# A hybrid residual block on one core: modulation columns of the first stage in two halves, and the output stage's rows and sums shared out anew

## The chip, the cores and the metric

The kernel runs on one core of one Trainium2 chip. The metric is the device time of one execution in microseconds. A run is compared by the median of its executions.

## The reference, cut to what matters

One residual block for a sequence of T = 1024 tokens with D = 1024 channels. Two places matter here, its beginning and its end:

```python
ada = jax.nn.silu(c) @ w_ada[l] + b_ada[l]              # c: (1, 1024), w_ada: (1024, 6144)
sh1, sc1, gt1, sh2, sc2, gt2 = jnp.split(ada, 6, axis=-1)
h = layer_norm(x, ln_in_g, ln_in_b)
u = h * (1.0 + sc1[:, None, :]) + sh1[:, None, :]
...                                                      # u @ w_in, mixers, router, experts
ff = hier_moe(...)                                       # two expert results per token, weighted and added
h = layer_norm(DEEPNORM_ALPHA * h + gt2[:, None, :] * ff, ln2_g[l], ln2_b[l])
return h
```

Between them stand the attention and delta-rule branches, the merge, the router and the experts, which take most of the time and which the change leaves alone.

## The kernel before

The kernel is a chain of stages in one program; each engine has its instruction list written out by hand, with semaphores between them, and a barrier of all engines ends a stage. The SyncE queue (SP) issues nearly all loads, in the order of the text, and a transfer that stands behind others in that queue lands behind them.

**First stage** (`prepare`, lines 225 to 439). It normalises x, computes the first two of the six modulation rows (shift and scale), turns the tokens into channels (the transposed `u`, split into two float16 parts) and sums the keys of the attention. SP loads x in four transfers, then the 8 MB of `w_ada` columns 0 to 2047 in five transfers of whole rows (L272), then the first piece of `w_in` (`load_dense(0)`: 256 key and value columns, L170, and 16 narrow columns, L171), then small tables, the rest of the constant table (L276) and the next piece of `w_in`. VectorE takes the statistics of all eight token tiles (L390), then one square root on ScalarE, then ScalarE normalises the eight tiles in place (L359). The shift row is summed on TensorE as a 1-row product: for each of 8 blocks k of 128 channels two matmuls with one column of weights (L295). The scale row is summed on VectorE (L404, L407), reduced over partitions by TensorE (L335), and both are turned into columns (L302, L335) and folded with the layer norm's weights into `modulation` by five small VectorE instructions (L414 to L421). Only when this is done for all 1024 channels may the first of sixteen steps n (channel block k = n // 2, token half n % 2) be modulated. A step is: `turn(n)`, four transposes on TensorE (L311); the modulation on ScalarE (L371, L373) for the even n and on VectorE (L427) for the odd n; a cast on ScalarE (L377) and a subtraction on VectorE (L433) that make the two float16 parts; and `keys(n)`, three matmuls (L321). After step 1 VectorE makes the low half of the first `w_in` piece (`split_dense_low`, L190, 2176 columns), and keys(0) waits for it. TensorE's order is ada of k = 0 to 5, three turns, ada of 6 and 7, the columns, then turn(n) and keys(n - 4) by turns. The product for the relative bias (L346) stands after keys(4) there.

**Output stage** (the end of `experts`). For each of eight tiles c of 128 tokens SP loads the two expert results (1 MB, L2274 to L2277, a ring of four); TensorE adds them into two PSUM banks with an identity matrix (L2415: eight passes of 512 columns a tile); VectorE multiplies the sum by the gate row into a buffer `gated` (L2602), adds the residual and takes the row sum (`sums`, L2605, L2607); ScalarE squares, takes the root (`moments`, L2514, L2516); VectorE makes the reciprocal and the shift, a product of two one-column operands (`scalars`, L2611, L2613); ScalarE makes the unit tile (`unit`, L2522); VectorE multiplies by the scale row and adds the shift row (`scale`, L2617, L2619); SP stores (L2280). VectorE's order is sums(c), scalars(c - 1), scale(c - 2). GpSimd has no work in this stage.

Of the kernel before, what the change touches and what calls it, by code (L numbers as in the profile page):

```python
# [15 lines left out]
P = 128  # L16
# [149 lines left out]
def load_dense(m, a, sp, i):  # L166

    w = a["w_in"][0].rearrange("(k p) n -> p k n", p=P)
    if i == 0:
        sp.dma_start(m.w_ring[:, 0, :, 0:2 * P], w[:, :, KB0:KB0 + 2 * P]).then_inc(m.w_in[0], 16)  # L170
        sp.dma_start(m.w_ring[:, 0, :, 2 * P:], w[:, :, BA0:BA0 + 16]).then_inc(m.w_in[0], 16)  # L171
    else:
        at = QB0 + (i - 1) * 2 * P if i < 5 else (i - 5) * 2 * P
        sp.dma_start(m.w_ring[:, i % 2, :, 0:2 * P], w[:, :, at:at + 2 * P]).then_inc(m.w_in[i % 2], 16)


def split_dense_high(nc, m, act, i, quarter=None):

    n = WIDE if i == 0 else 2 * P
# [5 lines left out]
def split_dense_low(nc, m, dve, i, quarter=None):  # L185

    n = WIDE if i == 0 else 2 * P
# [37 lines left out]
def prepare(nc, m, a):  # L225

    ROW = (1, 7)
    ON_TENSOR = 2
    GROUPED = ((0, 1), (2, 3), (4, 5), (6,), (7,))
    with ExitStack() as ctx:  # L230
# [4 lines left out]
        ada = m.sb("ada_early", [P, 2 * KC], ctx=ctx)  # L235
        ada_row = m.sb("ada_early_row", [1, D], ctx=ctx)
        part = m.sb("ada_early_partial", [P, D], ctx=ctx)
# [11 lines left out]
        wada_in = [m.sem(f"w_ada_in{n}") for n in range(len(GROUPED))]  # L249
        vecs_t, vecs_ok, sig_ok, silu_ok, ada_mm, part_ok, cols_mm = (m.sem(n) for n in (  # L250
            "vecs_transposed", "vecs_ready", "sig_c_ready", "silu_c_ready", "ada_summed", "ada_partial_ready", "ada_columns"))
        row_ok = [m.sem(f"ada_row_ready{n}") for n in range(2)]
# [12 lines left out]
        def _(sp):  # L265
# [19 lines left out]
        def _(pe):  # L285
# [6 lines left out]
            def ada(k):  # L292
                pe.wait_ge(wada_in[k // 2 if k < 6 else k - 3], 16)
                for n in range(ON_TENSOR):
                    last = pe.matmul(ps[0:1, ROW[n], :], m.silu_c[:, k:k + 1], wada[:, k, n * 512:(n + 1) * 512], start=(k == 0), stop=(k == KC - 1))  # L295
                    if k == KC - 1:
                        last.then_inc(ada_mm, 1)

            def columns(n):
                pe.wait_ge(row_ok[n], 1)  # L300
                for j in range(4 * n, 4 * n + 4):
                    last = pe.transpose(ps[:, 6, j:j + 1], ada_row[0:1, j * P:(j + 1) * P], m.const("ident")[0:1, 0:1])  # L302
                last.then_inc(cols_mm, 1)
# [10 lines left out]
            def keys(n):  # L314

                k, half = n // 2, n % 2
                if n == 0:
                    pe.wait_ge(m.w_lo, 4)
# [8 lines left out]
            for k in range(KC):  # L327
                ada(k)
                if k == KC - 3:
                    pe.wait_ge(z_ok, TC)  # L330
                    for n in range(3):
                        turn(n)
            pe.wait_ge(part_ok, 1)
            for j in range(KC):
                last = pe.matmul(ps[:, 6, KC + j:KC + j + 1], part[:, j * P:(j + 1) * P], m.const("ones")[:, 0:1], start=True, stop=True)  # L335
            last.then_inc(cols_mm, 1)
            for n in range(ON_TENSOR):
                columns(n)
            turn(3)
            for n in range(4, 2 * KC):  # L340
                turn(n)
                keys(n - 4)
                if n == 8:
                    pe.wait_ge(rel_in, 16)
                    pe.wait_ge(rest_in, 16)
                    pe.matmul(ps[0:QH, 7, 0:320], rel[:], m.const("one_hot", BUCKETS), start=True, stop=True).then_inc(bias_mm, 1)  # L346
            for n in range(2 * KC - 4, 2 * KC):
                keys(n)

        @block.scalar  # L350
        def _(act):
            act.wait_ge(vecs_ok, 1)
            nc.scalar.activation(sig_c[:], m.vec("c"), ACT.Sigmoid).then_inc(sig_ok, 1)
            act.wait_ge(var_ok, 1)
            nc.scalar.activation(std[:], mv[:, :, 1], ACT.Sqrt, bias=eps[:, 0:1]).then_inc(std_ok, 1)

            act.wait_ge(shift_ok, 1)
            for c in range(TC):
                nc.scalar.activation(x[:, c, :], x[:, c, :], ACT.Identity, scale=rstd[:, c:c + 1], bias=shift[:, c:c + 1]).then_inc(z_ok, 1)  # L359
            act.wait_ge(ada_mm, 1)  # L360
            nc.scalar.copy(ada_row[:, 0:512], ps[0:1, ROW[0], :]).then_inc(row_ok[0], 1)
            split_dense_high(nc, m, act, 0)

            act.wait_ge(ada_ok, 1)
            for n in range(2 * KC):
                k, half = n // 2, n % 2
                if half == 0:
# [12 lines left out]
        def _(dve):  # L380
# [5 lines left out]
            nc.vector.tensor_tensor(m.silu_c[:], sig_c[:], m.vec("c"), ALU.mult).then_inc(silu_ok, 1)  # L386
            for c in range(TC):
                dve.wait_ge(x_in[c // 2], 16)
                for s in range(2):
                    step(nc.vector.bn_stats(stats[:, c, s, :], x[:, c, s * 512:(s + 1) * 512]))  # L390
# [9 lines left out]
            for k in range(KC):  # L400
# [7 lines left out]
                if k < KC - 1:  # L408
                    step(last)
# [2321 lines left out]
```

## Time and profile before

| | |
|---|---|
| median of 3 runs (lowest, highest) | 1876.89 us (1872.59, 1880.91) |
| the profiled execution | 1877.39 us |
| its span | 1875.3 us |
| first stage, start to the barrier behind it | 0 to 67.4 us |
| output stage, last expert store to the end | 1815 to 1875.3 us |
| PE, DVE, ACT, POOL busy over the span | 93%, 76%, 56%, 20% |

Times in the trace are microseconds from the start of the span. PE is TensorE, DVE VectorE, ACT ScalarE, POOL GpSimd, SP SyncE; a "q" behind the name is the engine's queue, which issues transfers. "L2415" is line 2415 of the kernel. A timeline row gives start, duration, engine, line, operation, output<-input, count, and in brackets the idle time before it with what ended it. The chain of waits is followed back from the last instruction: what it waited for, and so on.

### The profile page before, as it was taken

What the parts mean: (1) busy time and instruction counts of PE and PEld (TensorE: products, weight loads), DVE (VectorE), ACT (ScalarE), POOL (GpSimd) and SP (SyncE); (2) the same over time, 40 slices, a digit from 0 to 9 for tenths busy, and PEclk for the clock granted to TensorE, in tenths of its full rate; (3) what the DMA queues carried; (4) which work ended last, traced back from release to release, by engine and by line L of the source; (5) the groups of instructions that cost most, each with busy time, mean ns of one, the idle gap of its engine ahead of it and who ended that gap; (6) DMA issues with size and microseconds to landing.
All of it is one profiled execution on the core that took longest, in us unless ns stands there. A gap on an engine that the chain in (4) does not pass through costs nothing. (4 is left out here: it accounts for less than half of the span.)

```text
span 1875.3 us, 35089 instructions
## 1 busy us (share of the span) xinstructions
PE 1739.5 (93%) x14040; PEld 968.8 (52%) x14040; DVE 1427.8 (76%) x1786; ACT 1057.4 (56%) x1336; POOL 375.2 (20%) x261
## 2 busy tenths in 40 slices
PE   4999999999969999989999998599999999999975
PEld 1656664444448888744444455344554455444432
DVE  5646577968777889456766688799999988988938
ACT  3455663454444445342334211488888888888834
POOL 0000000111113434200000000124544444445300
PEclk9999999999989999999999998699999999999987
DMA  8500018663456232061223121699999999999945
GB/s 341 103 29 24 23 41 312 239 205 105 179 131 155 66 92 53 2 216 57 85 84 113 45 90 56 261 390 393 408 408 409 408 400 402 394 395 382 366 153 196
DMA packets 160711, 385.05 MB, mean 205 GB/s; under 512 B 24859, under 2 KB 102292, under 8 KB 132670
## 3 DMA queue, kind: packets, MB, share of 16 engines
q1 hardware_dynamic: 145982, 351.58, 51.7%
q0 software_dynamic: 14592, 31.56, 4.4%
q8 instruction: 96, 1.57, 0.4%
q14 instruction: 41, 0.34, 0.1%
HBM read 354.86 MB, written 48.15 MB: 215 GB/s over the span
## 5 line engine op out<-in xcount | busy, mean ns | idle before, releaser
L2351 PE MATMUL ps<-w_gate_up_split,gathered_t 128*128 128x512 f16 x1680 | 378.8, 382 | 2.0 <-ACT gathered_t L2438 1.2
L2538 DVE SCALAR_TENSOR_TENSOR w_gate_up_split<-w_staged,w_gate_up_split 128x2048 f16<-128x2048 f32 x138 | 314.3, 2289 | 48.6 <-ACT w_gate_up_split L2429 47.1
L2429 ACT ACTIVATE w_gate_up_split<-w_staged 128x2048 f16<-128x2048 f32 x136 | 259.1, 1908 | 29.9 <-PE ps L2351 16.4
L2351 PEld LDWEIGHTS ps<-w_gate_up_split,gathered_t 128*128 128x128 f16 x1680 | 163.5, 99 | 197.3 <-issue 9.4
L219 PE MATMUL ps<-u_transposed,w_gates_split 128*128 128x512 f16 x1152 | 253.7, 382 | 4.7 <-PEq L144 3.1
L840 PE MATMUL ps<-u_transposed,w_dense_split 128*128 128x512 f16 x1104 | 240.2, 379 | 0.8 <-PEq L452 0.8
L219 PEld LDWEIGHTS ps<-u_transposed,w_gates_split 128*128 128x128 f16 x1152 | 113.1, 98 | 144.9 <-issue 12.1
L2378 PE MATMUL ps<-w_down_split,hidden_t 128*128 128x512 f16 x816 | 183.5, 381 | 0.8 <-ACT hidden_t L2475 0.6
L840 PEld LDWEIGHTS ps<-u_transposed,w_dense_split 128*128 128x128 f16 x1104 | 107.2, 98 | 135.5 <-issue 7.8
L2538 DVE SCALAR_TENSOR_TENSOR w_down_split<-w_staged,w_down_split 128x2048 f16<-128x2048 f32 x68 | 155.1, 2287 | 10.8 <-ACT w_down_split L2429 10.4
L2429 ACT ACTIVATE w_down_split<-w_staged 128x2048 f16<-128x2048 f32 x68 | 129.6, 1909 | 37.0 <-DMA w_staged<-in_w_down 21.5
L2378 PEld LDWEIGHTS ps<-w_down_split,hidden_t 128*128 128x128 f16 x816 | 78.4, 98 | 91.4 <-issue 2.5
L2308 POOL DMA_INDIRECT slots_scratch<-block_output,slot_row_now x35 | 47.1, 1346 | 321.0 <-ACT block_output L2447 290.3
L1772 ACT ACTIVATE gate_sigmoids<-ps 128x1024 f32<-128x1024 f32 x24 | 24.4, 1023 | 143.9 <-PE ps L219 143.8
L966 DVE SCALAR_TENSOR_TENSOR delta_output<-w_gates_split,vector_columns,delta_output 128x1024 f32<-128x1024 f32 x66 | 84.3, 1283 | 21.4 <-ACT delta_output L904 19.8
L501 PE MATMUL ps<-u_transposed,w_dense_split 128*128 128x512 f16 x384 | 91.0, 383 | 0.0
L1099 POOL DMA_DIRECT2D qkv_scratch<-delta_output x20 | 11.1, 554 | 366.1 <-ACT delta_output L911 366.1
L1706 PE MATMUL ps<-w_out_split,delta_output 128*128 128x512 f16 x384 | 84.0, 379 | 0.0
L2009 POOL COPY slot_token_now<-slot_tokens 128x2 uint32<-128x2 uint32 x1 | 0.2, 188 | 417.8 <-DVEq L2099 417.8
L2294 POOL DMA_INDIRECT gathered<-u_scratch,slot_token_now x33 | 75.6, 2290 | 28.1 <-POOL slot_token_now L2291 28.1
L2304 POOL COPY slot_row_now<-slot_rows_index 128x1 uint32 (+1 forms) x35 | 72.5, 2071 | 1.7 <-issue 1.6
L897 ACT ACTIVATE w_gates_split<-ps 128x1024 f32<-128x1024 f32 x24 | 24.5, 1019 | 84.2 <-PE ps L840 82.0
(367 smaller groups left out, 2949.0 us busy)
## 6 DMA issues: line engine op xcount, KB each, us to landing
w_staged<-in_w_gate SPq DMA_DIRECT2D x70, 1024.0 KB, 11.5
w_staged<-in_w_up SPq DMA_DIRECT2D x70, 1024.0 KB, 10.7
w_staged<-in_w_down SPq DMA_DIRECT2D x70, 1024.0 KB, 10.7
w_dense_ring<-in_w_in SPq DMA_DIRECT2D x17, 1024.0 KB, 7.8
w_ada_ring<-in_w_ada SPq DMA_DIRECT2D x8, 2048.0 KB
w_gates_ring<-in_w_in SPq DMA_DIRECT2D x24, 512.0 KB, 6.1
qkv_scratch<-delta_output POOLq DMA_DIRECT2D x20, 512.0 KB, 5.2
attention_output<-qkv_scratch SPq DMA_DIRECT2D x8, 1024.0 KB, 7.3
```

Source lines behind the costliest of these rows:

```text
L219: last = pe.matmul(m.ps[:, 2 * j + half, :], m.gate16[n % 2][:, j, wp, k, :], m.u[:, up, k, half * 512:half * 512 + 512], start=(t == 0), ...
L501: last = pe.matmul(ps[:, bank, :], w16[:, i % 2, wp, k, (j % 2) * P:(j % 2 + 1) * P], m.u[:, up, k, half * 512:half * 512 + 512], start=(t ...
L840: last = pe.matmul(ps[:, 2 * (1 - b) + half, :], w16[:, (FIRST + p) % 2, i, k, b * P:(b + 1) * P], m.u[:, j, k, half * 512:half * 512 + 51 ...
L966: last = nc.vector.scalar_tensor_tensor(acc[:, b, :], raw[:, b, 1 + t:1 + t + T], conv[:, t, n:n + 1], acc[:, b, :], ALU.mult, ALU.add)
L1706: last = pe.matmul(ps[:, y_bank(c) + half, :], merged(k, op)[:, c * P:(c + 1) * P], m.w_out[:, wp, k, half * 512:half * 512 + 512], start= ...
L2294: pool.indirect_dma_start(xg[:, s].rearrange("p h d -> p (h d)"), None, m.u2_dram.rearrange("t h d -> t (h d)"), bass.IndirectOffsetOnAxis ...
L2304: nc.gpsimd.tensor_copy(row[:, s:s + 1], m.slot_row[:, bass.ds(n, 1)]).then_inc(S("row_ready"), 1)
L2308: pool.indirect_dma_start(m.y_dram, bass.IndirectOffsetOnAxis(ap=row[:, s:s + 1], axis=0), y[:, s, :], None, bounds_check=2 * T - 1, oob_i ...
L2351: last = pe.matmul(ps[:, GU[s] + j, :], xt[:, s, xp, k, :], w16[:, j, wp, k, :], start=(k == 0 and t == 0), stop=(k == KC - 1 and t == 2))
L2378: last = pe.matmul(ps[:, 6 + half, :], ht[:, s, hp, k, :], w[:, wp, k, half * 512:half * 512 + 512], start=(k == 0 and t == 0), stop=(k == ...
L2429: nc.scalar.activation(split(kind, 0, int(q)), staged(m, kind, int(q)), ACT.Identity, scale=W_SCALE).then_inc(hi_ok[kind + q], 1)
L2538: nc.vector.scalar_tensor_tensor(split(kind, 1, int(q)), staged(m, kind, int(q)), W_SCALE, split(kind, 0, int(q)), ALU.mult, ALU.subtract) ...
```

## The change

In the first stage (the first diff; `GROUPED` is now two slices of four blocks, and the two pieces behind `if n == KC` stand in ScalarE's and in VectorE's loop over n) the modulation columns are loaded and used in two halves h of 512 columns of shift and 512 of scale (channel blocks k = 0 to 3, then 4 to 7). The products run on TensorE alone, as four matmuls side by side in groups of 32 output columns; ScalarE copies the bank, and a matmul with a small picking matrix, which GpSimd writes, sums two groups each and turns them. VectorE no longer sums the scale row. The layer norm goes by halves of tiles; the first `w_in` piece is loaded and split in two parts (128 key columns, then 144); TensorE's order is written anew, with the bias product before turn(10).

```diff
-            for n, ks in enumerate(GROUPED):
-                sp.dma_start(wada[:, ks[0]:ks[-1] + 1, :], w_view[:, ks[0]:ks[-1] + 1, 0:2 * D]).then_inc(wada_in[n], 16)
-            load_dense(m, a, sp, 0)
+            for h in range(HALVES):
+                for n, ks in enumerate(GROUPED):
+                    for part in range(2):
+                        cols = slice(part * D + h * 512, part * D + h * 512 + 512)
+                        sp.dma_start(wada[:, ks, cols], w_view[:, ks, cols]).then_inc(wada_in[h][n], 16)
+                load_first(m, a, sp, h)
...
+            def ada(h, j):
+                pe.wait_ge(wada_in[h][j // 2], 32)
+                for i in range(4):
+                    part, k = i // 2, 2 * j + i % 2
+                    last = pe.matmul(ps[32 * i:32 * i + 32, ROW[h], :], silu32[:, k, :], wada[:, k, part * D + h * 512:part * D + h * 512 + 512],
+                                     start=(j == 0), stop=(j == 3))
+            def columns(h):
+                pe.wait_ge(row_ok, h + 1)
+                for j in range(4):
+                    last = pe.matmul(ps[:, 6, 8 * h + 2 * j:8 * h + 2 * j + 2], ada_rows[:, h, j * P:(j + 1) * P], pick[:], start=True, stop=True)
...
+            ada(0, 0)
+            ada(0, 1)
+            pe.wait_ge(z_ok, TC // 2)
+            turn(0)
+            pe.wait_ge(z_ok, TC)
+            for n in range(1, 4):
                 turn(n)
+            ada(0, 2)
+            ada(0, 3)
+            columns(0)
+            turn(4)
+            turn(5)
+            keys(0)
+            turn(6)
+            keys(1)
+            turn(7)
+            keys(2)
+            for j in range(4):
+                ada(1, j)
+            turn(8)
+            turn(9)
+            columns(1)
+            pe.wait_ge(rel_in, 16)
+            pe.wait_ge(rest_in, 16)
+            pe.matmul(ps[0:QH, 7, 0:320], rel[:], m.const("one_hot", BUCKETS), start=True, stop=True).then_inc(bias_mm, 1)
+            turn(10)
+            keys(3)
+            turn(11)
+            keys(4)
+            keys(5)
+            for n in range(12, 2 * KC):
+                keys(n - 6)
+                turn(n)
+            for n in range(10, 2 * KC):
                 keys(n)
...
+                if n == KC:
+                    split_first_high(nc, m, act, 1)
+                    act.wait_ge(ada_mm, 2)
+                    nc.scalar.activation(ada_rows[:, 1, :], ps[:, ROW[1], :], ACT.Identity).then_inc(row_ok, 1)
...
+                if n == KC:
+                    split_first_low(nc, m, dve, 1)
+                if n % KC == 0:
+                    modulation(n // KC)
```

In the output stage TensorE copies the scale row into PSUM banks 0 and 1 once, and sums tiles 1 to 7 in the other six banks; VectorE sums tile 0 itself and keeps the gated sum in PSUM; GpSimd adds the shift row for tiles 0 to 6, VectorE for the last. (In the diff: GpSimd's loop, TensorE's, VectorE's `sums(c)` and `scale(c)`.) Tile 0's load is no longer in two parts, and the ring's slot 0 is freed by VectorE's sum.

```diff
+            for c in range(TC - 1):
+                pool.wait_ge(scaled_ok, c + 1)
+                nc.gpsimd.tensor_tensor(res[:, c % 3, :], res[:, c % 3, :], rows[:, 1, :], ALU.add).then_inc(res_ok, 1)
...
+            for half in range(2):
+                last = pe.matmul(ps[:, half, :], m.ident[:], rows[:, 0, half * 512:half * 512 + 512], start=True, stop=True)
+            last.then_inc(row_up, 1)
+            for c in range(1, TC):
+                pe.wait_ge(y_in[c % RING], 16 * (c // RING + 1))
+                if c >= 3:
+                    pe.wait_ge(sum_used, c - 2)
...
+                zc, yc = in_halves(m.z1[:, c, :]), ps[:, 2 + 2 * (c % 3):4 + 2 * (c % 3), :]
+                if c == 0:
+                    dve.wait_ge(y_in[0], 16)
+                    nc.vector.tensor_tensor(yc, in_halves(ys[:, 0, 0, :]), in_halves(ys[:, 0, 1, :]), ALU.add).then_inc(first_added, 1)
...
+                step(nc.vector.tensor_tensor(yc, yc, in_halves(rows[:, 2, :]), ALU.mult))
...
-                step(nc.vector.tensor_tensor(res[:, c % 3, :], res[:, c % 3, :], rows[:, 0, :], ALU.mult))
-                step.settle()
-                nc.vector.tensor_tensor(res[:, c % 3, :], res[:, c % 3, :], rows[:, 1, :], ALU.add).then_inc(res_ok, 1)
+                scaled = nc.vector.tensor_tensor(in_halves(res[:, c % 3, :]), in_halves(res[:, c % 3, :]), ps[:, 0:2, :], ALU.mult)
+                if c < TC - 1:
+                    scaled.then_inc(scaled_ok, 1)
+                else:
+                    step(scaled)
+                    step.settle()
+                    nc.vector.tensor_tensor(res[:, c % 3, :], res[:, c % 3, :], rows[:, 1, :], ALU.add).then_inc(last_ok, 1)
```

## Rows read from the trace of the kernel before

**Rows 1.** The page's head.

```profile
span 1875.3 us, 35089 instructions
```

**Rows 2.** Chain of waits, output stage: start, duration, engine, output, line.

```profile
1822.42 13.07 PE ps L2415 x24
...
1835.51 1.24 DVE gathered L2602
...
1840.85 1.14 DVE gathered L2602
...
1843.70 1.15 DVE w_staged L2617
...
1844.87 1.22 DVE w_staged L2619
...
1870.91 1.23 DVE w_staged L2619
```

**Rows 3.** Timeline of the first stage.

```profile
9.57 10.14 DVE L390 BATCH_NORM_STATS2 ln_stats<-attention_output 128x6 f32<-128x512 f32 x16 [2.91 <-DMA attention_output<-in_x]
...
21.27 9.16 ACT L359 ACTIVATE attention_output<-attention_output,ln_minus_mean_rstd,ln_rstd 128x1024 f32<-128x1024 f32 x8 [0.47 <-DVE ln_minus_mean_rstd L398]
...
22.21 8.51 PE L295 MATMUL ps<-w_ada_early,silu_c 128*1 128x512 f32 x16 [16.37 <-DMA w_ada_early<-in_w_ada]
...
36.82 3.59 PE L295 MATMUL ps<-w_ada_early,silu_c 128*1 128x512 f32 x8
...
37.30 0.42 SPq L276 DMA_DIRECT2D table<-in_table  x1
...
40.34 1.95 PE L335 MATMUL ps<-table,ada_early_partial 128*128 128x1 f32 x16
...
42.91 0.17 DVE L414 TENSOR_TENSOR ada_early<-ps,vector_columns 128x16 f32<-128x16 f32 x1 [1.78 <-PE ps L302]
...
43.80 0.78 ACT L371 ACTIVATE u_float<-ps,modulation 128x512 f32<-128x512 f32 x1 [1.72 <-DVE modulation L421]
...
46.56 2.42 DVE L190 SCALAR_TENSOR_TENSOR w_dense_split<-w_dense_ring,w_dense_split 128x2176 f16<-128x2176 f32 x1
...
49.03 1.46 PE L321 MATMUL ps<-u_transposed,w_dense_split 128*128 128x512 f16 x3 [2.96 <-DVE w_dense_split L190]
...
58.69 0.60 PE L311 MATMUL ps<-table,attention_output 128*128 128x128 f32 x4
...
59.77 0.60 PE L311 MATMUL ps<-table,attention_output 128*128 128x128 f32 x4
...
63.46 3.72 PE L321 MATMUL ps<-u_transposed,w_dense_split 128*128 128x512 f16 x15
```

**Rows 4.** Stretches: their length, PE, PEld, DVE, ACT, POOL busy, PEclk, DMA share, GB/s.

```profile
48.00:50.00 2.00, 0.97 (x3) 0.42 (x4) 2.00 (x3) 0.27 (x1) 0.00 (x0) 0.50 0.01 4
54.00:56.00 2.00, 2.00 (x13) 1.06 (x11) 1.64 (x3) 1.52 (x3) 0.00 (x0) 1.00 0.00 0
...
869.00:871.00 2.00, 2.00 (x11) 0.92 (x10) 2.00 (x1) 0.00 (x0) 0.00 (x0) 1.00 1.05 340
```

**Rows 5.** The page's transfer rate in 40 slices of the span.

```profile
GB/s 341 103 29 24 23 41 312 239 205 105 179 131 155 66 92 53 2 216 57 85 84 113 45 90 56 261 390 393 408 408 409 408 400 402 394 395 382 366 153 196
```

**Rows 6.** Timeline near 393 us, matmuls with 32 weight columns.

```profile
393.17 1.06 PE L851 MATMUL ps<-attention_output,table 128*32 128x512 f32 x8
```

**Rows 7.** One line of GpSimd: duration ns min/median/max.

```profile
L1557 POOL TENSOR_TENSOR w_and_q<-attention_output x32: 722/1011/1240, 547.0 to 770.6; 128x256 f32<-128x256 f32 x32
```

**Rows 8.** Timeline, 603 to 625 us: GpSimd and VectorE together.

```profile
602.95 0.69 DVE L1440 TENSOR_TENSOR level_parts<-minus_lower,table 128x512 f32<-128x512 f32 x1
...
622.77 1.89 POOL L1548 TENSOR_TENSOR state_decayed<-state,exp_g_last 128x1024 f32<-128x1024 f32 x1
...
622.80 0.41 DVE L1469 TENSOR_TENSOR inverse_t<-ps,inverse_t 128x256 f32<-128x256 f32 x1
...
623.46 1.75 DVE L1435 TENSOR_TENSOR decay_s<-decay_s,token_scalars 128x512 f32<-128x512 f32 x1
```

More of the change, by code:

```diff
@@ L227, in prepare @@
     ROW = (1, 7)
-    ON_TENSOR = 2
-    GROUPED = ((0, 1), (2, 3), (4, 5), (6,), (7,))
+    HALVES = 2
+    GROUPED = (slice(0, 4), slice(4, 8))
     with ExitStack() as ctx:
@@ L290, in _ @@
             pe.wait_ge(vecs_ok, 1)
[L292 to L302, printed above, removed]
+            def ada(h, j):
[4 more added lines that the diff above has]
+                                     start=(j == 0), stop=(j == 3))
+                if j == 3:
+                    last.then_inc(ada_mm, 1)
+            def columns(h):
+                pe.wait_ge(row_ok, h + 1)
+                for j in range(4):
+                    last = pe.matmul(ps[:, 6, 8 * h + 2 * j:8 * h + 2 * j + 2], ada_rows[:, h, j * P:(j + 1) * P], pick[:], start=True, stop=True)
                 last.then_inc(cols_mm, 1)
@@ L326, in _ @@
             pe.wait_ge(silu_ok, 1)
[L327 to L340, printed above, removed]
-                turn(n)
[L342 to L347, printed above, removed]
-                keys(n)
+            pe.wait_ge(pick_ok, 5)
+            ada(0, 0)
[4 more added lines that the diff above has]
+            for n in range(1, 4):
+                turn(n)
+            ada(0, 2)
[25 more added lines that the diff above has]
+            for n in range(10, 2 * KC):
+                keys(n)
+        @block.gpsimd
+        def _(pool):
+            nc.gpsimd.memset(pick[:], 0.0).then_inc(pick_ok, 1)
+            pool.wait_ge(pick_ok, 1)
+            for i in range(4):
+                nc.gpsimd.memset(pick[32 * i:32 * i + 1, i // 2:i // 2 + 1], 1.0).then_inc(pick_ok, 1)
         @block.scalar
@@ L385, in _ @@
             dve.wait_ge(sig_ok, 1)
[L386 to L390, printed above, removed]
-            step.settle()
-            for c in range(TC):
-                last = nc.vector.bn_aggr(mv[:, c, :], stats[:, c, :, :])
-            last.then_inc(var_ok, 1)
@@ L419, in _ @@
[L419 to L422 removed]
+            step(nc.vector.tensor_tensor(m.silu_c[:], sig_c[:], m.vec("c"), ALU.mult))
+            step.settle()
+            nc.vector.tensor_copy(silu32[:], m.silu_c[:].rearrange("p (k o) -> p k o", o=1).to_broadcast([P, KC, 32])).then_inc(silu_ok, 1)
@@ new lines, in _ @@
+            for g in range(2):
+                cs = slice(4 * g, 4 * g + 4)
+                for c in range(4 * g, 4 * g + 4):
+                    dve.wait_ge(x_in[c // 2], 16)
+                    for s in range(2):
+                        step(nc.vector.bn_stats(stats[:, c, s, :], x[:, c, s * 512:(s + 1) * 512]))
+                step.settle()
+                for c in range(4 * g, 4 * g + 4):
+                    last = nc.vector.bn_aggr(mv[:, c, :], stats[:, c, :, :])
+                last.then_inc(var_ok, 1)
+                dve.wait_ge(std_ok, g + 1)
+                step(nc.vector.reciprocal(rstd[:, cs], std[:, cs]))
+                step.settle()
+                nc.vector.scalar_tensor_tensor(shift[:, cs], mv[:, cs, 0], -1.0, rstd[:, cs], ALU.mult, ALU.mult).then_inc(shift_ok, 1)
```

152 lines of the change are left out of this document (77 added, 75 removed).

## The prediction

> **What bounds the kernel now.** The page's head gives the span, 1875.3 us [rows 1]; the profiled execution took 1877.39, so 2.1 us lie around the span. I read the chain of waits for the end of the kernel first. From 1835.51 to 1872.14 it holds nothing but VectorE: tile after tile, 5.24 us apart (1840.85 to 1844.87 + 1.22), and behind the last instruction 3.2 us for the last store [rows 2]. Before 1835.51 TensorE adds the first three tiles, 13.07 us for 24 passes, and VectorE waits. Then I read the timeline of the first stage [rows 3]. The modulation of the first channel block begins at 43.80. Ahead of it stand the last of `w_ada` (TensorE's last eight passes begin at 36.82, end 40.41), the columns (40.34 to about 42.9) and VectorE's five small instructions (42.91 to 43.77). Behind it the low half of the weights holds VectorE 2.42 us (46.56), keys(0) starts at 49.03, and the sixteen steps end with TensorE at 63.46 + 3.72 = 67.18. So the first stage is bound by the 8 MB of `w_ada` until 37 us, and then by a chain of steps that could have begun with half of it. What lies between the two stages doesn't change, and moves forward with the first stage's end.
>
> **First stage, step by step.** (1) Layer norm by halves. Sixteen statistics take 10.14 us, 0.63 each; the first scaled tile starts 1.55 after the last of them, 21.27 [rows 3]. With eight first: 9.57 + 5.07 + about 1.2 for the small ones = 15.8; the second half of the statistics follows then, and its four tiles (9.16 / 8 = 1.15 each) end at about 26.7, against 30.43.
> (2) Loads. 2 MB pieces landed from 22.21 and the last megabyte by 36.82: 6.3 MB in 14.6 us, 430 GB/s, in rows of 8 KB. The new pieces have rows of 2 KB. The experts' weights have such rows, and run at 400 to 409 [rows 5]. I take 405: the two pieces of h = 0 land at 22.5 and 27.7. The 128 key columns now stand in SP's queue ahead of h = 1, in rows of 512 bytes; a stretch that loads such rows runs at 340 [rows 4], so 0.5 MB costs 1.5 us, and h = 1 lands at 34.4 and 39.6. The rest of the table, for which the bias product waits, was issued at 37.30, just after `w_ada` had landed [rows 3]; it comes some 3 us later now, near 46, before it is wanted.
> (3) Products. Four matmuls with 32 weight columns each, eight passes, took 1.06 us together [rows 6], where eight passes with one column took 3.59 [rows 3]. So TensorE's 32 old passes become 64 that cost 8.5 us at the high clock, and twice that at the low one. ada(0, 0) and (0, 1) run from 22.5, at the low clock, to 26.7; turns 1 to 3 then end near 29 and (0, 2), (0, 3) at 31.2. ScalarE's copy 0.8 (as at 43.80), columns eight passes of 0.12 (1.95 / 16), VectorE 0.9: modulation starts at 33.9 instead of 43.80.
> (4) First four blocks. 2.76 to the split (43.80 to 46.56), which shrinks from 2176 to 1024 columns, 1.14: VectorE is free at 37.8, and three more blocks at 2 x 1.08 (58.69 to 59.77 is a step) end at 44.3, well before anything needs them.
> (5) TensorE's queue. keys(0) starts at 37.8. Three keys took 1.46 us a step at 49.03, when the granted clock was 0.50, that is 1.2 GHz, and 3.72 / 5 = 0.74 at 1.00 [rows 3, 4]. keys(0) to (2) with turns 6 and 7 cost 2.9 at the high level and 5.8 at the low one; idle gaps like those before 49.03 come again, so I take 4.5, to 42.3. Then the four ada(1, j), 4.2, to 46.5; copy 0.8, columns 1.0, VectorE 0.9. Turns 8 and 9 and the second split hide under these. The second half starts at 49.2, columns done at 48.3.
> (6) Second half. ScalarE and VectorE need 4 x 2.16, to 57.9. TensorE has more left: bias product 0.7, six steps of turn and keys at 1.08, seven keys at 0.74, together 12.4, to **60.7**. That is 6.5 less than 67.18. Ends: 8.5 if the clock stays high, 2 if it is low until 50. GpSimd's five fills of the picking matrix are short and done long before 22 us; ScalarE's and VectorE's wider copies of one small vector are in the 0.1s, under the loads.
>
> **Output stage.** (7) TensorE leaves out tile 0, but its first work now is tile 1, whose load is complete 1.5 MB after the half that started it at 1822.42, at 400 GB/s near 1826.3. The granted clock is low again after the idle time, so two tiles cost 16 passes at 0.43 plus the 2.75 that the 24 passes of 13.07 lost: tile 2 at 1835.9 instead of 1835.5. Nothing is won there: VectorE's own sum of tile 0 is hidden in its wait.
> (8) From there VectorE does L2617 but not L2619 for seven tiles: 7 x 1.24 = 8.7 less, and the pitch falls from 5.24 to 4.0. No row has VectorE writing PSUM; the nearest is L2602, which reads it and takes 1.14 [rows 2]. I take the same; 0.1 less or 0.3 more for each of six is -0.6 to +1.8. With the shift row gone from VectorE, ScalarE's chain for the last tile loses 1.2 us of cover, which comes back as waiting.
> (9) GpSimd. No row shows this addition. With one operand repeated, 1024 columns took 1.89 us [rows 8]; with two full operands, 256 columns took at least 0.72 [rows 7], four times which is 2.9. I take 2.3. It runs beside the next tile's multiply and sum (2.5 us), which read PSUM and one SBUF operand; at 622.80 such an instruction took 0.41 under a GpSimd one. One with two SBUF operands did not: L1435 took 1.75 instead of 0.69, to the end of GpSimd's [rows 8]. VectorE has two such left: the shift, one column, and the last tile's addition. The shift comes 2.9 us after the scale that starts GpSimd, so it is free in the steady part; behind tile 7 no sum stands between them, and it waits about 1.3, and the last addition 0.7. Whether one column is held too no row says: 0 to 2.0, and I take 2.0, as the nearest row was held to the end.
> The Trainium skill, SBUF — State Buffer, "SBUF: two separate sides", says that VectorE and GpSimd hold a shared pair of ports for a whole instruction, the other blocked. By that the 2.0 is due and the stage gains 5.2; without it 7.2.
> (10) Sum: -8.7 + 0.3 + 1.2 + 2.0 = **-5.2**. Stores follow as before, 3.2 us behind the last addition.
>
> **Total:** 6.5 + 5.2 = 11.7 off 1877.39 is 1865.7. The profiled execution lies 0.5 above the median of 1876.89, so I forecast 1865.2.
>
> **Rivals.** A, *TensorE slow in the middle.* The clock falls at the gaps before 37.8 and is low through ada(1): 4.2 for these and about 1.5 around them. Then 1871. For it: 0.50 at 48 to 50 [rows 4]; against it: the steady work from 37.8 on. 13%.
> B, *GpSimd sets the pace.* If its addition takes over 2.9 us, the shift waits at every tile. The median of L1557 is 1.011, four times which is 4.0 [rows 7]: 1.1 at each of four or five tiles and some 2 more at the end: the stage gains nothing, the kernel stands at 1871 to 1872. Against it: those 1.0 hold waits of their own. 12%.
> The Trainium skill, GPSIMD Engine Reference, "Performance versus the Vector engine", keeps element-wise work on VectorE: 4497 ns against 2293 for an addition of 2048 columns. An estimate from that is 2.2 us for 1024, under the point where B decides; rows 7 and 8, 1.89 to 2.9, agree with it.
> C, *slower: TensorE stays at 1.2 GHz through the whole first stage.* Its queue now holds the products, and the end hangs on it. Step 3 ends 3.1 later; from 40.9, sixteen keys at 1.46, ten turns at 0.68, ada(1) 8.5, columns and bias 3.4: 83.0, 15.8 later than now. Less 5.2: 1887.5. It decides only if the level never rises; at 54 to 56 it was 1.00 after five us of work [rows 4]. 4%.
> D, *the 32-column products do not run side by side.* 64 passes at 0.43 cost 27.5: some 19 more, 1884. Rows 6 speak plainly against it. 2%.
> E, *more.* The clock stays up and the one-column shift isn't held: 8.5 + 7.2, 1861.2. 14%.
> The forecast keeps 55%.
>
> **How the numbers follow.** A measurement of this kernel can tell about 0.5% from no change: 9.4 us, so 1867.5 and 1886.3 are the bounds. Of the forecast's 55% some 47 lie under 1867.5, with E and the lower edges of A and B 64% faster; C's upper part is 3% slower; the rest, 33%, is the same. The range reaches from E less a little, 1859.5, to B and A, 1872.5, and leaves out C, D and the far ends.
>
> **What would show it.** Right: ScalarE's first modulation (L371 before) near 34 instead of 43.80, the barrier near 61; eight 32-column passes in about 1.1; an output pitch of 4.0 with GpSimd rows of 2.3 that end before VectorE's one-column product; a long one-column product only behind tile 7. Wrong: granted clock 0.50 between 42 and 50, ScalarE waiting for `ada_summed` beyond 47; GpSimd rows over 2.9; a multiply into PSUM over 1.4; the bias product waiting for the table.

## The result, and the profile after

| | before | after |
|---|---|---|
| median (lowest to highest, runs) | 1876.01 us (1870.59 to 1880.91, 6) | 1861.85 us (1855.77 to 1865.02, 6) |
| the profiled execution, its span | 1877.39, 1875.3 us | 1865.02, 1863.2 us |

The ratio is 0.9924 [0.9906, 0.9941], so the kernel is faster by 0.6 to 0.9%, and 3.3 us under the forecast of 1865.2. The medians differ by 14.2 us, the two profiled executions by 12.4, their spans by 12.1. The profiled execution of after is the slowest of its six, so its trace shows the smaller difference.

I cut both spans at two points that exist in both: the end of TensorE's last keys (the first stage) and the end of TensorE's last expert pass (from there on it is the output stage). For the kernel before the first is 67.18 [rows 3]; the second is this row of its TensorE timeline, 1807.86 + 5.34 = 1813.20:

```profile
1807.86 5.34 PE L2378 MATMUL ps<-w_gate_up_split,hidden_t 128*128 128x512 f16 x24 [1.25 <-issue]
```

The same points of after, and the timeline around them (start, duration, engine, line, operation, output<-input, count, and in brackets the idle time before and what ended it). In this fence and in those below, rows between the ones shown are left out:

```profile
21.05 4.63 ACT L414 ACTIVATE attention_output<-attention_output,ln_minus_mean_rstd,ln_rstd 128x1024 f32<-128x1024 f32 x4 [0.44 <-DVE ln_minus_mean_rstd L462]
21.59 3.64 PE L326 MATMUL ps<-w_ada_early,silu_c 128*32 128x512 f32 x16 [15.79 <-DMA w_ada_early<-in_w_ada]
27.99 1.92 PE L326 MATMUL ps<-w_ada_early,silu_c 128*32 128x512 f32 x16
30.63 1.05 PE L334 MATMUL ps<-shift_and_scale_picked,ada_early_rows 128*128 128x2 f32 x8 [0.72 <-ACT ada_early_rows L416]
32.59 0.78 ACT L431 ACTIVATE u_float<-ps,modulation 128x512 f32<-128x512 f32 x1 [1.07 <-DVE modulation L475]
35.35 1.22 DVE L200 SCALAR_TENSOR_TENSOR w_dense_split<-w_dense_ring,w_dense_split 128x1024 f16<-128x1024 f32 x1
36.62 1.46 PE L353 MATMUL ps<-u_transposed,w_dense_split 128*128 128x512 f16 x3 [0.56 <-DVE w_dense_split L200]
41.56 3.64 PE L326 MATMUL ps<-w_ada_early,silu_c 128*32 128x512 f32 x32
46.95 0.71 PE L385 MATMUL ps<-table,rel_bias 32*16 32x320 f32 x2
54.79 4.05 PE L353 MATMUL ps<-u_transposed,w_dense_split 128*128 128x512 f16 x18
...
1799.36 5.34 PE L2441 MATMUL ps<-w_gate_up_split,hidden_t 128*128 128x512 f16 x24 [1.25 <-issue]
1804.53 1.88 PE L2470 MATMUL ps<-ln_gate_rows,identity 128*128 128x512 f32 x4
1817.41 26.82 PE L2478 MATMUL ps<-w_staged,identity 128*128 128x512 f32 x56 [11.00 <-DMA w_staged<-slots_scratch]
```

The modulation of the first channel block begins at 32.59 instead of 43.80, keys(0) at 36.62 instead of 49.03, and the last keys end at 54.79 + 4.05 = 58.84 instead of 67.18 [rows 3]. The last expert pass ends at 1799.36 + 5.34 = 1804.70. So:

| stretch | before | after | change | forecast |
|---|---|---|---|---|
| first stage | 67.18 | 58.84 | -8.3 | -6.5 |
| between | 1746.0 | 1745.9 | -0.2 | 0 |
| output stage | 62.1 | 58.5 | -3.6 | -5.2 |
| span | 1875.3 | 1863.2 | -12.1 | -11.7 |

(Between the two points it is 1746.02 before and 1745.86 after.) The sum came out nearly as forecast, but by luck: both terms are off, in opposite directions. The end of the timeline shows what the second one lost. VectorE and GpSimd in the last tiles:

```profile
1831.12 1.23 DVE L2672 TENSOR_TENSOR ps<-ps,ln_gate_rows 128x1024 f32<-128x1024 f32 x1
1831.29 2.36 POOL L2387 TENSOR_TENSOR w_staged<-w_staged,ln_gate_rows 128x1024 f32<-128x1024 f32 x1 [23.61 <-DVE w_staged L2688]
1835.11 1.23 DVE L2672 TENSOR_TENSOR ps<-ps,ln_gate_rows 128x1024 f32<-128x1024 f32 x1
...
1851.24 2.34 POOL L2387 TENSOR_TENSOR w_staged<-w_staged,ln_gate_rows 128x1024 f32<-128x1024 f32 x1 [1.64 <-DVE w_staged L2688]
1851.60 2.00 DVE L2682 TENSOR_TENSOR ln_minus_mean_rstd<-ln_minus_mean,ln_rstd 128x1 f32<-128x1 f32 x1
1854.80 2.35 POOL L2387 TENSOR_TENSOR w_staged<-w_staged,ln_gate_rows 128x1024 f32<-128x1024 f32 x1 [1.23 <-DVE w_staged L2688]
1856.16 2.07 DVE L2694 TENSOR_TENSOR w_staged<-w_staged,ln_gate_rows 128x1024 f32<-128x1024 f32 x1
1857.18 1.41 SPq L2339 DMA_DIRECT2D out<-w_staged  x2
```

The pitch, the time from one tile to the next, is 3.99 (1831.12 to 1835.11). VectorE's last addition ends at 1858.23; in the kernel before it ended at 1872.14 [rows 2]. Counted from the last expert pass that is 53.5 us instead of 58.9, 5.4 less. But the span ends 5.0 us behind it, where 3.2 lay before. In the trace each engine ends its work with a DRAIN row at the program's last line, before the closing barrier. These rows (engine's queue, instruction, count, duration ns min/median/max, start) and SP's waits (us in total, times, longest) say why:

```profile
L2707 POOLq DRAIN  x1: 8192/8192/8192, 1854.8 to 1854.8; - x1
L2707 SPq DRAIN  x1: 7/7/7, 1861.3 to 1861.3; - x1
```

```profile
SPq L2707 <- PEq L2707: 1.8, 1, 1.8
```

SP had seen its last store land and came to the closing barrier at 1861.3. GpSimd's drain began with the issue of its last addition and took 8.19 us, to 1863.0. The addition itself had ended at 1857.15, and the store that waits for it went out at 1857.18. So for 5.84 us GpSimd did nothing that the profile shows and still held the end up, 1.8 us longer than SP. The view of waits puts these 1.8 on a queue's name, PEq, that had long been done. In the kernel before the same drain stood in the shade, at 1818.2, behind GpSimd's last scatter (an indirect store):

```profile
L2632 POOLq DRAIN  x1: 5777/5777/5777, 1818.2 to 1818.2; - x1
```

### The profile page after: what moved, and what is told of

Read it like the earlier page. It is cut to its first block and busy times, and to the rows that moved or that the text cites. A ratio compares the mean times of both kernels' runs of the same rounds, so it can differ in the third digit from the quotient of the medians.

```text
span 1863.2 us, 35140 instructions
## 1 busy us (share of the span) xinstructions
PE 1731.0 (93%) x14060; PEld 968.2 (52%) x14060; DVE 1414.1 (76%) x1780; ACT 1059.0 (57%) x1339; POOL 394.8 (21%) x273
## 5 line engine op out<-in xcount | busy, mean ns | idle before, releaser
L1025 DVE SCALAR_TENSOR_TENSOR delta_output<-w_gates_split,vector_columns,delta_output 128x1024 f32<-128x1024 f32 x66 | 84.3, 1283 | 21.4 <-ACT delta_output L963 19.8
```

What stands on the lines that cost most here:

```text
L1025: last = nc.vector.scalar_tensor_tensor(acc[:, b, :], raw[:, b, 1 + t:1 + t + T], conv[:, t, n:n + 1], acc[:, b, :], ALU.mult, ALU.add)
```

## The experiments

Eleven kernels, one of them the change unaltered, ran beside the kernel before. The whole time of one execution moves by several us in the stretch between the two stages: between the same two points it took 1741.5 to 1750.0 us in kernels that do the same there. So a kernel that was timed only once is judged by its stage, from the last expert pass to the end of the span ("output stage"), or from the start of the first `columns` to the start of the last keys, and only the kernels with several executions by the whole. The output stage has a point of its own inside it, the start of VectorE's multiplication of tile 2. It lies 21.6 to 22.4 us behind the last expert pass in the eight profiles of the new output stage in which TensorE copies the scale row once. From there to the end of the span it takes 36.1 us (36.09 to 36.13) in the five profiles whose kernels do the same from there on. What an edit behind that point is worth is read against these 36.1.

**The two halves of the change.** Each alone: `first_stage_only` has the new first stage and the old `experts`, `output_stage_only` the reverse.

> The change's first stage with the output stage of before. Theory: the first stage's gain passes whole to the end. TensorE's last keys end near 58.8 us (67.2 before), the output stage lasts 62.1 us from TensorE's last expert pass to the end of the span, as before, and the span is about 1867, ratio 0.9955. Rival: a later stage that is bound by transfers waits for what now comes earlier, and gives part of the 8.3 us back: first stage 58.8, but span over 1870.

> The first stage of before with the change's output stage. Theory: VectorE ends 5.4 us earlier, but the end comes only 3.6 us earlier, since GpSimd's drain behind its last addition (8.2 us from its issue) now ends last: output stage 58.5 us instead of 62.1, span about 1871.7, ratio 0.998. Rival: the late end comes from the whole change or from this one profile: output stage about 56.7, span 1870.

Measured (4 and 10 executions), both against a median before of 1874.87: the first stage alone 1866.33, ratio 0.9952 [0.9935, 0.9968]; the output stage alone 1870.76, ratio 0.9977 [0.9967, 0.9986]. The product, 0.9929, is the 0.9924 of the whole change. With the first stage alone the last keys end at 57.94 and the output stage takes 62.3, as before; with the output stage alone it takes 58.3 (1867.2 - 1808.87) and GpSimd's drain is again the last to end (1858.8 + 8.19 = 1867.0, SP at 1865.4):

```profile
L2648 POOLq DRAIN  x1: 8189/8189/8189, 1858.8 to 1858.8; - x1
L2648 SPq DRAIN  x1: 7/7/7, 1865.4 to 1865.4; - x1
```

The two parts add up, within their intervals. Two thirds of the gain come from the first stage. No run takes that stage apart: how much the halves, the products on TensorE and the new order each give of it is read from rows below and not tested.

**What GpSimd's addition holds up on VectorE.** Three edits, one operand each. First the gated sum goes into SBUF instead of PSUM, so that the residual's addition has two SBUF operands:

```diff
-                step(nc.vector.tensor_tensor(yc, yc, in_halves(rows[:, 2, :]), ALU.mult))
+                yg = in_halves(gated[:, c % 2, :])
+                step(nc.vector.tensor_tensor(yg, yc, in_halves(rows[:, 2, :]), ALU.mult))
...
-                nc.vector.scalar_tensor_tensor(zc, yc, 1.0, zc, ALU.mult, ALU.add, accum_out=tot[:, 0, c:c + 1]).then_inc(sum_used, 1)
+                nc.vector.scalar_tensor_tensor(zc, yg, 1.0, zc, ALU.mult, ALU.add, accum_out=tot[:, 0, c:c + 1]).then_inc(sum_used, 1)
```

> The change with the gated sum written to SBUF as before, so that VectorE's addition of the residual has two SBUF operands. Theory (VectorE with two SBUF operands and GpSimd exclude each other): it starts 1.1 us into GpSimd's 2.36 us and is held to its end: 2.4 us instead of 1.22, the pitch of the output stage goes from 3.99 to about 5.1 and the stage grows by some 6 to 7 us. Rival (they share, or only GpSimd suffers): the addition stays under 1.4 us and the pitch under 4.2; GpSimd's additions may be longer.

Measured: 1872.18 us, output stage 1870.3 - 1806.80 = 63.5, 5.0 more than after, where 6 to 7 were expected, and 1.4 more than the kernel before. The line's rows, and two rows of its timeline:

```profile
L2676 DVE SCALAR_TENSOR_TENSOR u_transposed<-gathered,u_transposed x8: 1224/2342/2353, 1819.4 to 1854.3; 128x1024 f32<-128x1024 f32 x8
```

```profile
1848.10 2.35 POOL L2388 TENSOR_TENSOR w_staged<-w_staged,ln_gate_rows 128x1024 f32<-128x1024 f32 x1 [2.75 <-DVE w_staged L2690]
1849.19 2.34 DVE L2676 SCALAR_TENSOR_TENSOR u_transposed<-gathered,u_transposed 128x1024 f32<-128x1024 f32 x1
```

The same addition takes 1.22 alone and 2.34 beside GpSimd: GpSimd's ends at 1850.45, and VectorE's 1.08 later. GpSimd's own 2.35 does not change. The pitch is 5.11, as expected and hardly under the 5.24 of the kernel before. From tile 2 to the end it takes 41.7 us, 5.6 more than the 36.1. So the pairing of PSUM and GpSimd is what makes the steady part work: with the sum in SBUF the move of the shift row to GpSimd would have gained next to nothing in the pitch and, with the drain at the end, lost.

Then the scale row is read from SBUF instead of the banks:

```diff
-                scaled = nc.vector.tensor_tensor(in_halves(res[:, c % 3, :]), in_halves(res[:, c % 3, :]), ps[:, 0:2, :], ALU.mult)
+                scaled = nc.vector.tensor_tensor(in_halves(res[:, c % 3, :]), in_halves(res[:, c % 3, :]), in_halves(rows[:, 0, :]), ALU.mult)
```

> The change with VectorE's scaling reading the scale row from SBUF instead of the PSUM banks. Theory: in the steady part GpSimd's addition has ended 1.6 us before the next scaling starts, so nothing overlaps: pitch 3.99, scaling 1.22. Only the last scaling, which starts with GpSimd's last addition, is held (about 3.4 us instead of 1.22), and the last addition is then free (1.22 instead of 2.07): VectorE ends about 1.4 us later, the span within 0.7 us, since GpSimd's drain ends last. Rival (the banks matter at each tile): pitch 4.5 or more.

Measured: output stage 1858.3 - 1799.83 = 58.5, as after. The timeline of the end:

```profile
1848.59 1.21 DVE L2688 TENSOR_TENSOR w_staged<-w_staged,ln_gate_rows 128x1024 f32<-128x1024 f32 x1
1849.88 2.34 POOL L2387 TENSOR_TENSOR w_staged<-w_staged,ln_gate_rows 128x1024 f32<-128x1024 f32 x1 [1.23 <-DVE w_staged L2688]
1849.97 3.33 DVE L2688 TENSOR_TENSOR w_staged<-w_staged,ln_gate_rows 128x1024 f32<-128x1024 f32 x1 [0.17 <-ACT w_staged L2585]
1853.33 1.22 DVE L2694 TENSOR_TENSOR w_staged<-w_staged,ln_gate_rows 128x1024 f32<-128x1024 f32 x1
```

Seven of the eight scalings take 1.22 all the same, because no GpSimd addition runs at that moment; the eighth is held, 3.33, and the last addition behind it is no longer held. The sum of the two is 4.55, where after has 1.22 + 2.07; GpSimd's drain covers the difference. So the scale row in the banks is worth nothing as long as the drain sets the end.

Third, the one-column shift takes one of its factors as a scalar per partition instead of a second tensor:

```diff
-                nc.vector.tensor_tensor(shift[:, c:c + 1], mean[:, c:c + 1], rstd[:, c:c + 1], ALU.mult).then_inc(shift_ok, 1)
+                nc.vector.tensor_scalar(shift[:, c:c + 1], mean[:, c:c + 1], rstd[:, c:c + 1], None, ALU.mult).then_inc(shift_ok, 1)
```

> The change with VectorE's one-column product written with the reciprocal as a per-partition scalar, so that it has one SBUF tensor operand. Theory: what holds it behind tile 7 is the second tensor operand: it falls from 2.00 us to about 0.15, GpSimd's last addition starts 1.0 us earlier, its drain too, and the output stage (TensorE's last expert pass to the end of the span) is 57.5 us instead of 58.5. Rival: any small VectorE instruction on SBUF is held, whatever its operands: 2.0 us as before, stage 58.5.

Measured: output stage 1860.6 - 1803.41 = 57.2, 1.3 less than after. The line's rows, and VectorE's last two scalings and its last addition:

```profile
L2682 DVE TENSOR_SCALAR ln_minus_mean_rstd<-ln_minus_mean,ln_rstd x8: 213/214/214, 1824.6 to 1850.0; 128x1 f32<-128x1 f32 x8
```

```profile
1850.95 2.36 DVE L2688 TENSOR_TENSOR w_staged<-w_staged,ps 128x1024 f32<-128x1024 f32 x2 [0.72 <-ACT w_staged L2585]
1853.34 2.34 DVE L2694 TENSOR_TENSOR w_staged<-w_staged,ln_gate_rows 128x1024 f32<-128x1024 f32 x1
```

None of the eight is held any more; in after the eighth took 2.00. From tile 2 to the end the stage takes 35.3, so the edit is worth 0.8; the other 0.5 lies ahead of tile 2. The edit is worth no more because the drain still ends the stage, 8.19 us behind the issue of GpSimd's last addition, and that came, counted from tile 2, only 0.7 earlier: the scaling of tile 6 in front of it now waits 0.72 for ScalarE's unit tile, and the new form costs 0.21 in each tile instead of 0.16. VectorE's last addition, with two SBUF operands, is held as before, 2.34. The Trainium skill, SBUF — State Buffer, "SBUF: two separate sides", says that a VectorE instruction with two SBUF inputs and a GpSimd instruction exclude each other for their whole length. The traces agree: 2.34 in `gated_in_sbuf`, 3.33 in `scale_row_in_sbuf` and 2.00 in after, where the form alone takes 1.22, 1.22 and 0.16.

**The drain.** Tile 6 is summed by VectorE too, so that GpSimd's last addition is that of tile 5 (two of the three places that name the last tile):

```diff
-            for c in range(TC - 1):
+            for c in range(TC - 2):
                 pool.wait_ge(scaled_ok, c + 1)
...
-                if c < TC - 1:
+                if c < TC - 2:
                     scaled.then_inc(scaled_ok, 1)
```

> The change with the shift row of tile 6 added by VectorE too, so that GpSimd ends one tile earlier. Theory: the drain of 8.2 us follows GpSimd's last addition and moves with it, some 3.6 us earlier, off the end; VectorE ends within 0.4 us of where it ended, because the last addition is no longer held; the last store then ends the span: output stage about 56.9 us. Rival: the late end isn't GpSimd's drain but the end of the program itself: stage 58.5, drain as late as before relative to the end.

Measured: output stage 1857.0 - 1801.06 = 55.9, 2.6 less than after.

```profile
L2707 POOLq DRAIN  x1: 8187/8187/8187, 1846.8 to 1846.8; - x1
L2707 SPq DRAIN  x1: 7/7/7, 1856.8 to 1856.8; - x1
```

The drain is as long as before, but it starts earlier, ends at 1855.0, and SP closes the span. VectorE does one addition more (1.22), the last one is not held (1.22 instead of 2.07), and the last shift is still held (2.00). VectorE's end, 1853.93, lies 52.9 us behind the last expert pass, 0.7 less than in after. But here tile 2's multiplication began 0.8 sooner, and counted from it VectorE ends 0.15 later than in after. From tile 2 to the end it takes 34.3, so the edit is worth 1.8 of the 2.6, and all of it is the drain, whose cost hangs on where GpSimd's last instruction stands.

**The clock.** The granted clock (PEclk) is given as a share of 2.4 GHz; 0.50 is 1.2 GHz. After has TensorE at rest from 1806.41 to 1817.41 and then in part at 1.2 GHz, as this window shows (its length, PE, PEld, DVE, ACT, POOL busy, PEclk, DMA share, GB/s):

```profile
1817.00:1823.00 6.00, 5.59 (x7) 2.38 (x8) 1.78 (x4) 2.82 (x4) 0.00 (x0) 0.54 1.02 410
```

Here TensorE multiplies the scale row seven times instead of once:

```diff
-            for half in range(2):
+            for half in 7 * (0, 1):
                 last = pe.matmul(ps[:, half, :], m.ident[:], rows[:, 0, half * 512:half * 512 + 512], start=True, stop=True)
```

> The change with TensorE's copy of the scale row into PSUM done seven times instead of once, to keep TensorE at work until tile 1 has landed. Theory: tile 1 and 2 are summed at the low clock (9.67 us for 16 passes), and this sets when VectorE's run begins; at the high clock it is 6.9, and the output stage is 2.7 us shorter, 55.8. Rival: the loads of tiles 1 and 2 or VectorE's own tile 0 stand behind it: under 1 us.

Measured: output stage 1853.7 - 1797.83 = 55.9, 2.6 less. TensorE's timeline, and a window of the stretch:

```profile
1797.67 12.18 PE L2470 MATMUL ps<-ln_gate_rows,identity 128*128 128x512 f32 x28
1810.41 24.30 PE L2478 MATMUL ps<-w_staged,identity 128*128 128x512 f32 x56 [0.56 <-DMA w_staged<-slots_scratch]
```

```profile
1810.00:1818.00 8.00, 7.59 (x18) 3.52 (x19) 4.94 (x11) 3.94 (x6) 0.00 (x0) 1.00 1.03 410
```

The granted clock is 1.00 in the window, and the 56 passes take 24.30 instead of 26.82. Tile 2's multiplication begins 19.8 us behind the last expert pass instead of 22.4, and from there to the end it takes 36.1 as in after: the whole gain lies ahead of it.

The same in the first stage: three more matmuls, six passes into a bank that is not yet in use, behind the first `columns`.

```diff
             columns(0)
+            for _ in range(3):
+                pe.matmul(ps[:, 7, :], m.const("ident"), x[:, 0, 0:512], start=True, stop=True)
             turn(4)
```

> The change with three extra matmuls behind the first columns in the first stage, whose result is overwritten, so that TensorE isn't idle there. Theory: keys(0) to (2), which ran at 1.2 GHz in the change, run at 2.4, the products of the second half end 2 us earlier, and the first stage ends 1.5 us earlier, at 57.3, the rest hidden behind the weights' split. Rival: the second half waits for its loads or the split anyway, or the clock falls all the same: first stage within 0.5 of 58.8.

Measured: 1863.11 us, which alone says nothing. The same windows of after, and then of this kernel:

```profile
32.00:36.00 4.00, 1.91 (x8) 1.57 (x8) 3.15 (x8) 3.31 (x5) 0.00 (x0) 0.74 1.05 409
36.00:40.00 4.00, 3.44 (x11) 1.83 (x11) 3.84 (x6) 2.47 (x4) 0.00 (x0) 0.50 0.79 194
40.00:44.00 4.00, 4.00 (x32) 1.79 (x34) 2.88 (x5) 3.15 (x5) 0.00 (x0) 0.90 0.90 256
```

```profile
32.00:36.00 4.00, 2.63 (x15) 1.48 (x14) 3.26 (x6) 2.57 (x6) 0.00 (x0) 1.00 1.05 410
36.00:40.00 4.00, 4.00 (x35) 1.93 (x37) 3.71 (x6) 3.80 (x6) 0.00 (x0) 1.00 0.97 221
40.00:44.00 4.00, 3.67 (x36) 2.14 (x28) 3.05 (x5) 2.32 (x4) 0.00 (x0) 1.00 0.92 297
```

The granted clock no longer falls in these windows, and from the first `columns` to the last keys it takes 22.66 us (29.29 to 51.95) instead of 24.16; the nine profiles without the fill have 23.3 to 24.8. In this kernel the bias product waited 0.45 for its table, so the load is near to setting the pace there.

**All together.** Three kernels timed side by side (6, 6 and 5 executions): the change unaltered; the change with the three edits that shortened the output stage (tile 6, the shift by a scalar, the row seven times); and these with the fill of the first stage.

> The changed kernel once more, unaltered, timed beside the two that follow. From the middle of the first comparison: ratio to the kernel before 0.992 (0.990 to 0.994), output stage (TensorE's last expert pass to the end of the span) 58.5 us, GpSimd's drain about 8.2 us from the issue of its last addition and the last thing but one to end. Its first stage shows the low clock again between 30 and 40 us, and from the first columns to the last keys some 24 us.

> Three changes to the output stage together: tile 6 summed by VectorE, the shift's second factor as a scalar operand, and the scale row multiplied seven times so that TensorE does not rest before the tiles come. Theory: they take three different things (GpSimd's drain and the held last addition: -2.6 in the run with tile 6 alone; the hold on the 128x1 product: -1.3; the low clock under the first tiles: -2.6), so they add up: output stage 58.5 - 6.5 = 52.0 us, 53 if the hold moves to another instruction in part; ratio about 0.989. The first rival is that they overlap, because the loads of the staged tiles set the pace once TensorE is at 2.4 GHz: then the stage stays at 55 to 56, as with the seven products alone. The second rival is that GpSimd's drain ends the span again: it lay 1.8 us ahead of SP's in the run with tile 6, so a VectorE chain that ends over 1.8 us earlier without GpSimd's last addition moving earlier would give 54.

> The kernel with the three changes to the output stage, and six more products (three calls of two passes) behind the first columns, so that TensorE does not rest there. Theory: the low clock from 32 to 44 us goes, and from the start of the first columns to the start of the last keys it takes 22.7 us where the kernels without the fill take 23.4 to 24.2; so the whole is 0.7 to 1.5 us shorter than the kernel with the three output changes, ratio to it 0.9992 to 0.9996 (hardly to be told from 1 by the times; the interval within the trace is what decides). Rival: the loads of the weights bind in the middle of this stage, and the interval is the same 23.4 to 24.2.

| | median | ratio to before (1875.33) | first columns to last keys | output stage |
|---|---|---|---|---|
| after_again | 1858.68 | 0.9908 [0.9893, 0.9922] | 23.34 | 58.4 |
| output_three | 1855.58 | 0.9887 [0.9869, 0.9905] | 24.81 | 53.4 |
| combined | 1854.52 | 0.9884 [0.9868, 0.9900] | 22.14 | 53.3 |

The last one's rows:

```profile
1793.19 5.34 PE L2443 MATMUL ps<-w_gate_up_split,hidden_t 128*128 128x512 f16 x24 [1.25 <-issue]
```

```profile
L2709 POOLq DRAIN  x1: 8199/8199/8199, 1842.5 to 1842.5; - x1
L2709 SPq DRAIN  x1: 7/7/7, 1851.6 to 1851.6; - x1
```

The output stage takes 53.3 to 53.4 instead of 58.4: 5.1 less, where the three edits gave 6.5 one by one. Neither rival explains the missing 1.4: the tiles' loads did not hold it at 55, and the drain ends well before SP (1850.7 and 1851.6 in the last kernel). The multiplication of tile 2 does, which TensorE's sum releases. Its rows in after, `shift_by_scalar`, `tile6_on_vector` and `combined`:

```profile
1827.11 1.23 DVE L2672 TENSOR_TENSOR ps<-ps,ln_gate_rows 128x1024 f32<-128x1024 f32 x1 [0.48 <-PE ps L2478]
1825.28 1.23 DVE L2672 TENSOR_TENSOR ps<-ps,ln_gate_rows 128x1024 f32<-128x1024 f32 x1 [0.42 <-PE ps L2478]
1822.66 1.23 DVE L2672 TENSOR_TENSOR ps<-ps,ln_gate_rows 128x1024 f32<-128x1024 f32 x1 [0.48 <-PE ps L2478]
1818.13 1.23 DVE L2674 TENSOR_TENSOR ps<-ps,ln_gate_rows 128x1024 f32<-128x1024 f32 x1 [0.43 <-PE ps L2480]
```

That is 22.4, 21.9, 21.6 and 19.6 us behind the last expert pass. So 0.5 of the scalar's 1.3 and 0.8 of tile 6's 2.6 were no gain of the edits but an earlier sum in that one execution, 1.4 together. What the edits do themselves adds up: 0.8 for the scalar, 1.8 for tile 6 and 2.6 for the seven products are 5.2. Why the sum comes 21.6 to 22.4 us behind the last expert pass in kernels that do the same up to there isn't shown.

Of the fill the trace shows 1.2 us against `after_again` and 2.7 against `output_three` in its own stretch, at a granted clock of 1.00 from 28 to 44; the medians (1855.58 and 1854.52) can't tell it from nothing. The combined kernel's median lies 20.8 us under the kernel before and 4.2 under the change. The intervals of these two ratios still overlap a little, but four of its five executions are shorter than the shortest of the change's six.

## Why the prediction was right, and which steps were off

**First stage: right in the mechanism, 1.9 us too small.** Step (1): the second half of the tiles ends at 21.05 + 4.63 = 25.7; forecast 26.7. Step (2): the first products began at 21.59, when their load landed, not at 22.5. The next two pairs, expected to land at 27.7, ran without a wait for a load at 27.99 here and at 26.06 in `after_again`, so there that load was at least 1.6 us sooner than I put it. Step (3): the first sixteen passes of the 32-column products took 3.64, the next sixteen 1.92, where I had 4.2 and 2.1; the modulation began at 32.59, forecast 33.9. The rows give for this 0.9 by the landing and 0.6 and 0.2 by the products, less some 0.5 by the turns between them. Step (4): the split of 1024 columns took 1.22, forecast 1.14. Step (5): keys(0) at 36.62, forecast 37.8; from there to ada(1) 4.94 us, forecast 4.5, at a granted clock of 0.74, 0.50 and 0.90 (windows above), and ada(1) 3.64, forecast 4.2. Step (6): from the bias product to the end 11.9, forecast 12.4. Together: 1.2 earlier to start with, 0.4 lost to the clock, 0.6 and 0.5 won back: 58.84 instead of 60.7. The largest miss is the load's landing in (2), 0.9 us at the head of the chain. After's profile is even the latest of its kind: the eight other profiles with this first stage and no fill ended it at 56.1 to 57.9, and their first `columns` began at 28.7 to 29.7, here at 30.63. But the landing moves with the execution and not only with the edit. `output_stage_only` has the old first stage, and there the first piece is used from 20.47 instead of 22.21, and the stage ends at 65.91 instead of 67.18:

```profile
20.47 8.99 PE L295 MATMUL ps<-w_ada_early,silu_c 128*1 128x512 f32 x16 [14.47 <-DMA w_ada_early<-in_w_ada]
62.19 3.72 PE L321 MATMUL ps<-u_transposed,w_dense_split 128*128 128x512 f16 x15
```

Against this one the eight gain 8.0 to 9.8 us, so the 6.5 was too small by more than one pair of profiles shows.

**Output stage: VectorE's end as forecast, in part by luck, the end of the span not.** Step (7): tile 2's sum was ready 22.4 us behind the last expert pass (1817.41, and 9.67 for 16 passes in the chain of waits), forecast 22.7. Step (8): pitch 3.99, forecast 4.0; the multiply into PSUM took 1.23, where I had taken 1.14. Step (9): GpSimd's addition 2.36, forecast 2.3. The estimate from the Trainium skill, GPSIMD Engine Reference, "Performance versus the Vector engine", was 2.2. No VectorE row is held in the steady part. Behind tile 7 two waits were forecast to make 2.0 together, 1.3 for the shift and 0.7 for the last addition. The shift took 2.00 instead of 0.16 and the last addition 2.07 instead of 1.22, so the holds were 1.84 and 0.85, 2.7 together. The 1.2 that ScalarE's chain was to cost in step (8) came to 0.4: in the tail VectorE waited 0.24 for ScalarE's root and 0.18 for its unit tile. The two errors nearly cancel, 3.1 against 3.2. By the figures of step (7) the 0.3 in (10) should be 0.4 (1835.9 against 1835.5). VectorE's end moved by -5.4, forecast -5.2. What failed for the span is one sentence of step (10), "Stores follow as before, 3.2 us behind the last addition": the end of the span was taken from SP alone, while GpSimd's drain, hidden in the kernel before, moved with GpSimd's work to the very end. It took 1.8 back.

**Rivals.** A and C: the low clock came in the windows between 32 and 44, but ada(1) ran at 0.91 for eight passes, the rate of the high level. The first sixteen passes took 1.82 for eight, at a granted clock that the view gives as 1.00; what slowed them isn't shown. B: GpSimd needs 2.36, and the pace is VectorE's. D: 0.91 to 0.96 for eight passes, side by side. E: the first stage came near its 8.5, but not for E's reason, as the clock did fall; and the shift was held. `fill_behind_columns` and `shift_by_scalar` show that a clock that stays up and a shift that isn't held were each to be had by an edit, the second for 0.8 us and not for the 2.0 that E gives it, as the drain still set the end.

## What to carry to other kernels

When work moves to another engine at the end of a program, look at what that engine still has to do before the program may end, not only at the instruction: here 5.8 us of drain that had been hidden for free. Beside a GpSimd instruction on SBUF keep one operand of every VectorE instruction in PSUM or in a scalar, down to a single column: what had two SBUF operands here was held to GpSimd's end. And compare stages, from one common point to the next, when the whole moves by more than the effect; put the common point right ahead of the edit, or a sum that happens to come 0.8 us sooner is taken for a gain.

## What was not expected of the hardware

GpSimd's drain at the end of the program took 8.18 to 8.20 us from the issue of its last 2.35 us addition in eleven profiles, wherever that stood, and 5.78 us behind a scatter in the two with the old output stage. The low clock in the output stage had been forecast (2.75 us; it cost 2.5 over the 56 passes). That it could be avoided had not: with 24 passes whose result was not needed the granted clock was 1.00, with no loss elsewhere that the trace shows.
